# A two-network forward pass on one NeuronCore: side work of the delta-rule and sparse-attention branches moved by two to four places along the weight stream

## The chip, the core and the metric

The kernel runs on one core of one Trainium2 chip. The core has TensorE (PE, matrix products; its loading of weights is shown apart as PEld), VectorE (DVE), ScalarE (ACT), GpSimd (POOL) and SyncE (SP, which issues most transfers). The metric is the device time of one execution in microseconds; lower is better.

## The reference

Two networks run one after the other on the same 256 tokens of width 1024, each with two layers. The second one is the one that matters here. The core of its layer:

```python
h = rmsnorm(x, norm_mix[l])
(dq, dk, dv, dz, db, da, sq, sk, sv, iq, ik, iw, xq, gl) = jnp.split(h @ w_in[l], split_pts, axis=-1)
o_dn = deltanet_branch(dq, dk, dv, dz, db, da, conv_w[l], a_log[l], dt_bias[l], dn_norm[l])
o_sa = dsa_branch(sq, sk, sv, iq, ik, iw, positions)
o_xa = memory_branch(xq, rmsnorm(mem, norm_mem[l]), w_mem_kv[l])
gates = jax.nn.sigmoid(gl + b_gate[l])
merged = gates[:, :, 0] * (o_dn @ w_branch[l, 0]) + gates[:, :, 1] * (o_sa @ w_branch[l, 1]) + ...
x = x + merged @ w_out[l]
```

deltanet_branch: a causal convolution of width 4 and silu on q, k, v; per head (8 of them) and chunk of 64 tokens a unit lower triangular system is solved, and a state is carried from chunk to chunk; the output is normalised and multiplied by silu(z). dsa_branch: an index product relu(iq ik) weighted and summed over 8 index heads gives a score, the best 64 keys of each query are selected, and attention runs over these alone; q, k and iq carry a rotary embedding. memory_branch: plain attention over 256 memory rows. A gated feed-forward network follows. Everything is float32.

## The kernel before, in words

**The weight stream.** TensorE's main work is one long stream of matrix products with weights from device memory. A weight arrives in halves of 128x1024. Each is split in two: ScalarE writes the high part (w_hi, L339), GpSimd the remainder (w_lo, L348), and TensorE forms three products (x_hi w_hi, x_lo w_hi, x_hi w_lo; L147 to L149). A half is two parts of 12 matmuls of 256 columns (6 of 512 where the output is laid out by tokens, as in sv). Before w_hi of a half may be written, an earlier half's product must be done, since the buffers for halves are a ring.

**Units.** Halves are grouped into units, each with a target bank of PSUM and a follow-up on ScalarE or VectorE. In a layer of the second network, counted in halves from sm: sm 0-1; q0, q1, k0, k1, v0, v1, z0, z1 (2-17, first head half); q2 to z3 (18-33, second head half); sq 34-41; sk 42-49; iq 50-53; sv0 54-57; sv1 58-61; then gates and branch products by turns, gl00 62-63, wb00 64-65, gl01 66-67, wb01 68-69 and so on, and xq from 78. A part number is twice the half's.

**Side work.** All else on TensorE (the chunk solve, scan, index product, scores, transposes) is set between parts by hand. `main.pe(pe, n)` issues the stream up to part n; `main.act(...)` and `main.dve(...)` do the same for the follow-ups on their engines, so that the written order is the order in each engine's queue. An engine works through its queue in that order and waits on semaphores. For the delta rule `places` (L1541) makes a table of part numbers from a start and a list of gaps, one for each head half; the names are the steps: spread, spread_e, k0 ... g1 (preparation), lower (transposes of the start of the solve, two groups g of four head-chunks), y1, c1 ... y5, c5 (five levels of the solve, a product and a masked cross product each), solved, w0, o0 ... w3, o3 (scan of four chunks), tail0, tail1 (transposes of the result for two token tiles; its high and low part are o_dn_hi and o_dn_lo). For the sparse attention `self.at(half)` gives the places: index (L1804), scores (L1819), turn (L1831), weighted (L1841). On VectorE, index_sum (L2340) sums the eight index heads in eight operations into sc, index_mask (L2354) takes the best keys by repeated maximum and replacement; its dictionary says after which rounds the stream's follow-ups are issued and up to which half.

**Hooks.** The convolution of a q, k or v unit is two ScalarE operations and six of VectorE (L1384). The rotary embedding of sq, sk and iq is a small matmul two halves after the unit's end and three VectorE operations (L1575) three halves after it; iq1's stands at part 114. branch_unit adds gated products into acc on VectorE (L1489, "merged(k,n)"), which frees the bank of wb for the next one.

**Tables.** ScalarE needs a table load when it changes between function sets (Silu, Ln and Exp, and so on). `preload_act_table_set` puts one at a chosen place.

Of the kernel before, what the change touches and what calls it, by code (L numbers as in the profile page):

```python
# [1320 lines left out]
class Mixer2:  # L1321


    def __init__(self, net, l):
# [110 lines left out]
        for t in ("sq", "sk"):  # L1435
            for i in range(4):
                plain(f"{t}{i}", m[t][:, 2 * i:2 * i + 2, :], 5 - i % 2, rope=(j, "perm128", cs[:, 0, :], sn[:, 0, :]))
                j += 1
        for i in range(2):
            plain(f"iq{i}", m["iq"][:, 2 * i:2 * i + 2, :], 5 - i % 2, rope=(j, "perm64", cs[:, 1, :], sn[:, 1, :]))  # L1440
            j += 1
        for c in range(2):
            token_unit(f"sv{c}", m["sv"][:, :, c * HALF:(c + 1) * HALF], [4 + 2 * c, 5 + 2 * c], xs)
        u["sv1"].need = u["sv1"].need + [("rot_read", l, 9), ("rot_read", l, 10)]

# [82 lines left out]
        self.units = [u[n] for n in self.order]  # L1528
        self.steps = [self.places(0, 32), self.places(1, 76)]

# [10 lines left out]
    def places(self, hf, start):  # L1541

        gaps = ([("spread", 0), ("spread_e", 2 if hf == 0 else 1), ("k0", 2 if hf == 0 else 1), ("k1", 1), ("v0", 1), ("v1", 1), ("q0", 1), ("q1", 1), ("beta", 1),
                 ("g0", 1), ("g1", 1), ("lower0", 2), ("lower1", 1)] + [(f"{n}{lv}", 1) for lv in range(1, 6) for n in ("y", "c")]
                + [("solved", 1)] + [(f"{n}{c}", g) for c in range(NCH) for n, g in (("w", 2), ("o", 1))]
                + [("tail0", 4), ("tail1", 1)])
        at, out = start, {}
        for name, gap in gaps:
            at += gap
            out[name] = at  # L1550
        return out
# [35 lines left out]
    def pe(self, pe):  # L1587
# [28 lines left out]
        for hf in range(2):  # L1616
            self.prepare_pe(pe, hf)
            self.solve_pe(pe, hf)
            self.scan_pe(pe, hf, key_sum)
        self.index_pe(pe, 0, 60)  # L1620
        main.pe(pe, self.at(65))
        self.scores_pe(pe, 0)
        self.scores_pe(pe, 1)
        self.index_pe(pe, 1, 66)
        main.pe(pe, self.at(69))
        self.scores_pe(pe, 2)
        self.scores_pe(pe, 3)
        self.turn_pe(pe, 0)
        self.turn_pe(pe, 1)
        main.pe(pe, self.at(71))  # L1630
        self.weighted_pe(pe, 0)
        self.weighted_pe(pe, 1)
        main.pe(pe, self.at(78))
        self.turn_pe(pe, 2)
        main.pe(pe, self.at(79))
        self.turn_pe(pe, 3)
        main.pe(pe, self.at(80))
        self.weighted_pe(pe, 2)
        main.pe(pe, self.at(81))
        self.weighted_pe(pe, 3)  # L1640
        main.pe(pe, self.at(83))
        for g in (0, 1, 2):
# [80 lines left out]
    def solve_pe(self, pe, hf):  # L1723
        net, l, sig = self.net, self.l, self.net.sig
        K, main, m, bank = net.K, net.main, net.mem2, net.bank
        h = m["half"]
        yd, cp = bank[0:2], bank[2:4]
        for g in range(2):
            main.pe(pe, self.step_at(hf, f"lower{g}"))
            pe.wait_ge(*sig.at("begun", l, hf, g))  # L1730
            for n in range(4 * g, 4 * g + 4):
                mm = pe.transpose(yd[g][:, (n % 4) * P:(n % 4 + 1) * P], h["ti"][:, n, :], K("ident"))
            mm.then_inc(*sig.up("begun_turned", l, hf, g))
# [151 lines left out]
    def act(self, act):  # L1885
# [31 lines left out]
        for hf in range(2):  # L1917
            self.chain_act(act, hf, key_log)
        main.act(act, self.at(60))
        self.index_act(act, 0)  # L1920
        main.act(act, self.at(66))
        self.exponentials(act, 0)
        self.exponentials(act, 1)
        self.index_act(act, 1)
        main.act(act, self.at(69))
        self.turned_copy(act, 0)
        self.turned_copy(act, 1)
        main.act(act, self.at(71))
        self.weighted_high(act, 0)
        self.weighted_high(act, 1)  # L1930
        main.act(act, self.at(75))
        self.exponentials(act, 2)
        self.exponentials(act, 3)
        main.act(act, self.at(78))
        self.turned_copy(act, 2)
        main.act(act, self.at(79))
        self.turned_copy(act, 3)
        main.act(act, self.at(80))
        self.weighted_high(act, 2)
        act.preload_act_table_set("natural_log_exp_and_others")  # L1940
        for tt in range(TT):
# [28 lines left out]
    def chain_act(self, act, hf, key_log):  # L1970
# [4 lines left out]
        act.wait_ge(*sig.at("diffed", l, hf))  # L1975
        act.activation(h["e"][:, :, :], h["e"][:, :, :], ACT.Exp).then_inc(*sig.up("decay_made", l, hf))
        for g in range(2):
            main.act(act, self.step_at(hf, f"lower{g}"))
            act.wait_ge(*sig.at("begun_turned", l, hf, g))
            act.activation(h["t"][:, 4 * g:4 * g + 4, :], bank[g][:, :].rearrange("p (n i) -> p n i", n=4), ACT.Copy  # L1980
                           ).then_inc(*sig.up("t_begun", l, hf, g))
# [5 lines left out]
        for c in range(NCH):  # L1987
# [81 lines left out]
    def dve(self, dve):  # L2069
# [43 lines left out]
        for hf in range(2):  # L2113
            self.prepare_dve(dve, hf, unit_key)
            self.solve_dve(dve, hf)
            self.scan_dve(dve, hf, unit_key)
        main.dve(dve, self.at(60))
        self.index_sum(dve, 0)
        self.index_mask(dve, 0, {})
        main.dve(dve, self.at(65))  # L2120
        self.weigh(dve, 0)
        self.weigh(dve, 1)
        main.dve(dve, self.at(66))
        self.normalise(dve, 0)
        self.normalise(dve, 1)
        self.index_sum(dve, 1)
        self.index_mask(dve, 1, {1: 70})
        for g in (0, 1):
            self.weighted_low(dve, g)
        self.weigh(dve, 2)  # L2130
        main.dve(dve, self.at(74))
        self.weigh(dve, 3)
        self.normalise(dve, 2)
        self.normalise(dve, 3)
        dve.wait_ge(*sig.at("mem_loaded", l))
        bn, mv, ms = m["mem_bn"], m["mem_mv"], m["mem_ms"]
        for tt in range(TT):
            for half in range(2):
# [4 lines left out]
                                     ).then_inc(*sig.up("mem_var", l, tt))  # L2143
        main.dve(dve, self.at(80))
        self.weighted_low(dve, 2)
        for tt in range(TT):
            dve.wait_ge(*sig.at("mem_root", l, tt))
            dve.tensor_scalar(m["mem"][:, tt, :], m["mem"][:, tt, :], m["mem_rs"][:, tt:tt + 1], None, ALU.mult
                              ).then_inc(*sig.up("mem_normed", l, tt))
        main.dve(dve, self.at(81))  # L2150
        self.weighted_low(dve, 3)
        main.dve(dve, self.at(83))
        gain = prm(l, "norm_mem")
# [105 lines left out]
    def solve_dve(self, dve, hf):  # L2259
# [443 lines left out]
```

## Time and profile before

| | us |
|---|---|
| time, median of 3 runs | 2277.57 (2274.91 to 2277.58) |
| the profiled execution, its own time | 2277.58 |
| its span in the profile | 2275.8 |
| PE busy | 2163.2 (95%) |
| POOL busy | 1498.6 (66%) |
| ACT busy | 1073.0 (47%) |
| DVE busy | 955.9 (42%) |

The first network takes about 650 us. The attention part of the second network's first layer runs from 651 to 1075 us of the span, and the second layer's a little over 800 us later. Busy times are of the whole span. The granted clock is TensorE's share of full speed (2.4 GHz).

### The profile page before, as it was taken

The page shows a single profiled execution, that of the slowest core. Times are in us where ns is not written, and L with a number is a line of the kernel's source. Part 1 is how long each engine was busy: PE and PEld are TensorE (multiplying, and loading weights), DVE is VectorE, ACT ScalarE, POOL GpSimd, SP SyncE. Part 2 cuts the span into 40 slices and gives each one's busy share as a digit, 9 for nine tenths or more (in the row PEclk, how much of TensorE's full clock was granted, in tenths as well). Part 3 has the DMA queues.
Part 4 walks back from the last instruction along what each step waited for, and adds up shares of the span by engine and source line. Part 5 has one row for each costly group of instructions (what it writes and reads, how often), then busy time and mean ns, then how long its engine had stood idle before and what let it go on. Part 6 is the DMA issues. An engine that isn't in the chain of part 4 may idle for free.

```text
span 2275.8 us, 35984 instructions
## 1 busy us (share of the span) xinstructions
PE 2163.2 (95%) x15336; PEld 2001.3 (88%) x15336; DVE 955.9 (42%) x1484; ACT 1073.0 (47%) x1517; POOL 1498.6 (66%) x632
## 2 busy tenths in 40 slices
PE   8989989899969899999999899998999999999998
PEld 7789978799959888989999899898889899998998
DVE  4353256442375537477112211456374681123112
ACT  4555555555545352255444444473441454544444
POOL 6679877698846234356778688663243566786886
PEclk9999999999989999999999999999999999999999
DMA  8345544355524113134445455442131344454553
GB/s 338 132 146 204 185 139 161 117 180 187 184 84 147 60 71 106 64 128 167 151 164 185 148 185 185 156 145 90 56 112 56 130 148 149 157 182 150 184 185 133
DMA packets 47183, 333.05 MB, mean 146 GB/s; under 512 B 5168, under 2 KB 5552, under 8 KB 7856
## 3 DMA queue, kind: packets, MB, share of 16 engines
q1 hardware_dynamic: 47024, 330.76, 41.9%
q8 instruction: 121, 1.98, 0.4%
q14 instruction: 38, 0.31, 0.0%
HBM read 329.69 MB, written 1.05 MB: 145 GB/s over the span
## 4 chain that ended last, share of the span: by engine, by line
PE 62%; DVE 8%; issue 1%; ACT 1%; POOL 0%; DVEq 0%; ACTq 0%
PE bank L147 14%; PE bank L149 14%; PE bank L148 14%; PE y L147 2%; PE y L149 2%; PE y L148 2%; PE bank L1749 2%; PE bank L1748 1%; PE bank L1739 1%; DVE conv L1384 1%; PE bank L1672 1%; PE bank L1794 1%; PE bank L1791 1%; PE bank L1774 1%; DVE sq L1583 1%
## 5 line engine op out<-in xcount | busy, mean ns | idle before, releaser
L348 POOL TENSOR_TENSOR w_lo<-w_raw,w_hi 128x1024 fp32r<-128x1024 f32 x602 | 1463.0, 2437 | 759.7 <-ACT w_hi L339 759.6
L339 ACT ACTIVATE w_hi<-w_raw 128x1024 fp32r<-128x1024 f32 x602 | 635.7, 1059 | 1009.4 <-PE bank L149 838.9
L147 PE MATMUL bank<-x_hi,w_hi 128*128 128x256 f32 x2960 | 876.6, 296 | 21.6 <-POOL w_lo L348 17.1
L148 PE MATMUL bank<-x_lo,w_hi 128*128 128x256 f32 x2960 | 848.4, 287 | 0.0
L149 PE MATMUL bank<-x_hi,w_lo 128*128 128x256 f32 x2960 | 848.3, 287 | 0.0
L147 PEld LDWEIGHTS bank<-x_hi,w_hi 128*128 128x128 f32 x2960 | 579.1, 196 | 44.9 <-issue 24.4
L148 PEld LDWEIGHTS bank<-x_lo,w_hi 128*128 128x128 f32 x2960 | 579.0, 196 | 10.5 <-issue 8.6
L149 PEld LDWEIGHTS bank<-x_hi,w_lo 128*128 128x128 f32 x2960 | 578.4, 195 | 0.0
L876 DVE SCALAR_TENSOR_TENSOR conv<-bank,par_sb,conv 128x254 f32<-128x254 f32 (+1 forms) x176 | 76.8, 478 | 240.1 <-ACT conv L864 238.6
L1246 DVE TENSOR_TENSOR hid_lo<-hid,hid_hi 128x512 fp32r<-128x512 f32 x22 | 45.1, 2048 | 241.2 <-ACT hid_hi L1241 241.2
L147 PE MATMUL y<-w_hi,hid_hi 128*128 128x512 f32 x352 | 139.9, 397 | 3.3 <-DVE hid_lo L898 3.3
L149 PE MATMUL y<-w_hi,hid_lo 128*128 128x512 f32 x352 | 138.9, 395 | 0.0
L148 PE MATMUL y<-w_lo,hid_hi 128*128 128x512 f32 x352 | 138.9, 395 | 0.0
L1384 DVE SCALAR_TENSOR_TENSOR conv<-bank,par_sb,conv 128x255 f32<-128x255 f32 (+1 forms) x144 | 62.6, 477 | 63.8 <-ACT conv L1375 62.1
L147 PEld LDWEIGHTS y<-w_hi,hid_hi 128*128 128x128 f32 x352 | 66.3, 188 | 19.2 <-DVE hid_lo L898 5.4
L149 PEld LDWEIGHTS y<-w_hi,hid_lo 128*128 128x128 f32 x352 | 66.2, 188 | 15.7
L148 PEld LDWEIGHTS y<-w_lo,hid_hi 128*128 128x128 f32 x352 | 66.2, 188 | 13.8
L1491 DVE SCALAR_TENSOR_TENSOR gate<-gate,bank 128x512 f32<-128x512 f32 x16 | 11.0, 688 | 130.5 <-PE bank L149 130.5
L1749 PE MATMUL bank<-ti,es 128*128 128x128 f32 x320 | 61.0, 290 | 4.1 <-DVE es L2275 4.1
L1748 PE MATMUL bank<-es,ti 128*128 128x128 f32 x256 | 51.8, 286 | 7.0 <-DVE es L2275 7.0
L1749 PEld LDWEIGHTS bank<-ti,es 128*128 128x128 f32 x320 | 49.6, 205 | 4.5 <-DVE es L2275 4.5
L2347 DVE SCALAR_TENSOR_TENSOR sc<-index,tokq,sc 128x128 f32<-128x128 f32 (+1 forms) x28 | 52.6, 1878 | 1.0
(397 smaller groups left out, 3243.6 us busy)
## 6 DMA issues: line engine op xcount, KB each, us to landing
w_raw<-w SPq DMA_DIRECT2D x300, 1024.0 KB, 4.8
ln_rows<-ln_rows SPq DMA_DIRECT2D x4, 1024.0 KB, 7.2
mem_tok<-mem SPq DMA_DIRECT2D x2, 1024.0 KB, 4.9
const_sb<-const SPq DMA_DIRECT2D x1, 1536.0 KB, 9.3
par_sb<-par SPq DMA_DIRECT2D x2, 553.5 KB, 10.7
xn<-xT SPq DMA_DIRECT2D x1, 1024.0 KB, 4.9
w_raw<-w SPq DMA_DIRECT2D x2, 512.0 KB, 5.4
x_tok<-x SPq DMA_DIRECT2D x1, 1024.0 KB, 7.2
```

The lines of the kernel that those rows point to most:

```text
L147: pe.matmul(out, lhs[0], rhs[0], start=start, stop=False, skip_group_check=skip)
L148: pe.matmul(out, lhs[0], rhs[1], start=False, stop=False, skip_group_check=skip)
L149: return pe.matmul(out, lhs[1], rhs[0], start=False, stop=stop, skip_group_check=skip)
L339: act.activation(self.hi[:, h % HALVES, :], self.raw[:, n % RAWS, i * HW:(i + 1) * HW], ACT.Copy).then_inc(*sig.up("high", h))
L348: pool.tensor_tensor(self.lo[:, h % HALVES, :], self.raw[:, n % RAWS, i * HW:(i + 1) * HW], self.hi[:, h % HALVES, :].bitcast(F32), ALU.su ...
L876: ins = dve.scalar_tensor_tensor(cb[:, j, tap:T], view[:, j, 0:T - tap], taps[:, 2 - tap, c0 + j:c0 + j + 1], cb[:, j, tap:T], ALU.mult, A ...
L1246: dve.tensor_tensor(net.hs2[1][:, 2 * (i % 3):2 * (i % 3) + 2, :], m["hid"][:, i % 2, :, :], net.hs2[0][:, 2 * (i % 3):2 * (i % 3) + 2, :] ...
L1384: ins = dve.scalar_tensor_tensor(cb[:, j, tap:T], two(b)[:, j, 0:T - tap], taps[:, 3 - tap, c0 + j:c0 + j + 1], cb[:, j, tap:T], ALU.mult, ...
L1583: net.dve_chain.step(dve.tensor_tensor(raw, raw, cos.unsqueeze(1).to_broadcast([P, w, T]), ALU.mult))
L1748: pe.matmul(yd[g][:, c], h["ti"][:, n, :], h["y"][:, n, :], start=True, stop=True)
L1749: mm = pe.matmul(cp[g][:, c], h["y"][:, n, :], h["ti"][:, n, :], start=True, stop=True)
L2347: ins = dve.scalar_tensor_tensor(sc, m["r"][qt][:, (h % 2) * 4 + h // 2, :], m["tokq"][:, qt, 4, h:h + 1], mask if h == 0 else sc, ALU.mul ...
```

## The change

Places of the first head half start at part 30 and not 32, those of the second at 73 and not 76. The transposes of the solve, lower0 and lower1, become one place, lower, so that everything from y1 on is one part closer still. The banks of sq, sk and iq change from 5, 4 to 4, 5 by turns. sv1 no longer waits for the last two rotations to be read. Index product, scores, turn and weighted steps move to earlier halves. On ScalarE a call that issues the stream's follow-ups up to one part before tail0 is put ahead of the table preload of the tail. On VectorE index_mask(1) issues follow-ups at three rounds and not one, the call for half 66 before normalise(0) becomes 64, and that before weigh(3) moves behind normalise(2).

```diff
-                plain(f"{t}{i}", m[t][:, 2 * i:2 * i + 2, :], 5 - i % 2, rope=(j, "perm128", cs[:, 0, :], sn[:, 0, :]))
+                plain(f"{t}{i}", m[t][:, 2 * i:2 * i + 2, :], 4 + i % 2, rope=(j, "perm128", cs[:, 0, :], sn[:, 0, :]))
...
-        u["sv1"].need = u["sv1"].need + [("rot_read", l, 9), ("rot_read", l, 10)]
...
-        self.steps = [self.places(0, 32), self.places(1, 76)]
+        self.steps = [self.places(0, 30), self.places(1, 73)]
...
-                 ("g0", 1), ("g1", 1), ("lower0", 2), ("lower1", 1)] + [(f"{n}{lv}", 1) for lv in range(1, 6) for n in ("y", "c")]
+                 ("g0", 1), ("g1", 1), ("lower", 2)] + [(f"{n}{lv}", 1) for lv in range(1, 6) for n in ("y", "c")]
...
-        self.index_pe(pe, 0, 60)
-        main.pe(pe, self.at(65))
+        self.index_pe(pe, 0, 58)
+        main.pe(pe, self.at(63))
         self.scores_pe(pe, 0)
         self.scores_pe(pe, 1)
-        self.index_pe(pe, 1, 66)
-        main.pe(pe, self.at(69))
+        self.index_pe(pe, 1, 64)
+        main.pe(pe, self.at(67))
         self.scores_pe(pe, 2)
         self.scores_pe(pe, 3)
         self.turn_pe(pe, 0)
         self.turn_pe(pe, 1)
-        main.pe(pe, self.at(71))
+        main.pe(pe, self.at(69))
...
+        main.pe(pe, self.step_at(hf, "lower"))
         for g in range(2):
-            main.pe(pe, self.step_at(hf, f"lower{g}"))
...
+        main.act(act, self.step_at(hf, "tail0") - 1)
         act.preload_act_table_set("natural_log_exp_and_others")
...
-        main.dve(dve, self.at(66))
+        main.dve(dve, self.at(64))
         self.normalise(dve, 0)
         self.normalise(dve, 1)
         self.index_sum(dve, 1)
-        self.index_mask(dve, 1, {1: 70})
+        self.index_mask(dve, 1, {1: 66, 4: 69, 6: 70})
         for g in (0, 1):
             self.weighted_low(dve, g)
         self.weigh(dve, 2)
-        main.dve(dve, self.at(74))
         self.weigh(dve, 3)
         self.normalise(dve, 2)
+        main.dve(dve, self.at(75))
         self.normalise(dve, 3)
```

The later places (78 to 83 on three engines) move down by one half, the ScalarE and VectorE calls in step with TensorE's.

VectorE's queue in the first layer, from the maxima of weigh(1) to the first round of index_mask(1), before:

```order
L2379 TENSOR_SCALAR mx_190<-mx_190 128x4
L1489 SCALAR_TENSOR_TENSOR merged<-gate_171,bank 128x512
L2385 RECIPROCAL rc_192<-sum_191 128x4
L2386 TENSOR_TENSOR sm_0_158<-sm_0_158,rc_192 128x512
L2385 RECIPROCAL rc_192<-sum_191 128x4
L2386 TENSOR_TENSOR sm_1_159<-sm_1_159,rc_192 128x512
L2347 SCALAR_TENSOR_TENSOR sc<-index_154,tokq,const_sb 128x256
L2347 SCALAR_TENSOR_TENSOR sc<-index_154,tokq,sc 128x256 x7
L2362 MAX m_189<-sc 128x8
L2363 MATCH_REPLACE wk<-m_189,sc 128x256
L1489 SCALAR_TENSOR_TENSOR merged<-gate_171,bank 128x512
```

The first merged is merged(0,0), the second merged(0,1). The same stretch of VectorE's queue after the change:

```order
L2379 TENSOR_SCALAR mx_190<-mx_190 128x4
L2385 RECIPROCAL rc_192<-sum_191 128x4
L2386 TENSOR_TENSOR sm_0_158<-sm_0_158,rc_192 128x512
L2385 RECIPROCAL rc_192<-sum_191 128x4
L2386 TENSOR_TENSOR sm_1_159<-sm_1_159,rc_192 128x512
L2347 SCALAR_TENSOR_TENSOR sc<-index_154,tokq,const_sb 128x256
L2347 SCALAR_TENSOR_TENSOR sc<-index_154,tokq,sc 128x256 x7
L2362 MAX m_189<-sc 128x8
L2363 MATCH_REPLACE wk<-m_189,sc 128x256
L1488 SCALAR_TENSOR_TENSOR merged<-gate_171,bank 128x512
```

merged(0,0) has moved behind the sum and the first round; merged(0,1) comes three rounds later.

VectorE's queue at the end of the second head half, a piece of the difference (the rope of iq1 against the tail and the first index sum):

```order
 L2326 TENSOR_TENSOR mt<-vb,o_ms 128x512 x2
-L1582 TENSOR_TENSOR rope_148<-bank,tables 128x512
-L1583 TENSOR_TENSOR iq<-iq,tables 128x512
-L1585 TENSOR_TENSOR iq<-iq,rope_148 128x512
+L1581 TENSOR_TENSOR rope_148<-bank,tables 128x512
+L1582 TENSOR_TENSOR iq<-iq,tables 128x512
+L1584 TENSOR_TENSOR iq<-iq,rope_148 128x512
 L2332 SCALAR_TENSOR_TENSOR o_turned<-bank,par_sb,z_set_112 128x512 x2
 L2338 TENSOR_TENSOR o_dn_lo<-o_turned,o_dn_hi 128x4x128 x2
+L1581 TENSOR_TENSOR rope_148<-bank,tables 128x512
+L1582 TENSOR_TENSOR iq<-iq,tables 128x512
+L1584 TENSOR_TENSOR iq<-iq,rope_148 128x512
```

Ahead of the tail stood the rope of iq1 and stands now that of iq0; iq1's is the last of the piece, behind o_dn_lo.

ScalarE's queue at the end of the first head half, from the last copy of the scan on, after the change:

```order
L1994 ACTIVATE vb<-bank 64x512
L1998 ACTIVATE mt<-vb 128x512
L339 ACTIVATE w_hi<-w_raw 128x1024
L1399 ACT_TABLE_LOAD
L1399 ACTIVATE z_set_112<-bank 128x512
L339 ACTIVATE w_hi<-w_raw 128x1024
L2001 ACT_TABLE_LOAD
L2005 ACTIVATE o_ms<-o_ms,const_sb 128x4
L2008 ACTIVATE o_ms<-o_ms 128x4
```

And before:

```order
L1995 ACTIVATE vb<-bank 64x512
L1999 ACTIVATE mt<-vb 128x512
L2001 ACT_TABLE_LOAD
L2005 ACTIVATE o_ms<-o_ms,const_sb 128x4
L2008 ACTIVATE o_ms<-o_ms 128x4
```

The Silu of z3 (z_set_112), its table load and two w_hi stand between the scan and the tail's table load now; before, the same Silu was issued ahead of the last vb copy.

## Rows read from the trace of the kernel before

**Rows 1.** The page, part 1: busy us, share of span, instructions.

```profile
PE 2163.2 (95%) x15336; PEld 2001.3 (88%) x15336; DVE 955.9 (42%) x1484; ACT 1073.0 (47%) x1517; POOL 1498.6 (66%) x632
```

**Rows 2.** Waits of PE, 651 to 1075: us in total, times, longest.

```profile
PE bank L1732 <- DVE ti L2256: 5.3, 2, 3.1
...
PE bank L1748 <- DVE es L2275: 3.5, 2, 2.0
PE bank L147 <- DVE merged L1489: 2.6, 2, 1.4
PE bank L1749 <- DVE es L2275: 2.0, 1, 2.0
PE bank L1785 <- DVE v_new L2304: 1.7, 1, 1.7
```

**Rows 3.** Stretches: length, busy us (instructions) by engine, PEclk, DMA share, GB/s.

```profile
703.00:857.00 154.00, 143.59 (x1051) 134.84 (x1050) 75.64 (x134) 72.65 (x100) 58.34 (x25) 0.92 0.24 81
857.00:990.00 133.00, 130.78 (x956) 116.62 (x954) 81.78 (x117) 38.97 (x52) 50.99 (x22) 1.00 0.26 90
1080.00:1105.00 25.00, 25.00 (x212) 25.00 (x212) 0.00 (x1) 11.45 (x14) 20.69 (x9) 1.00 0.49 169
1512.00:1666.00 154.00, 143.66 (x1059) 134.44 (x1058) 75.85 (x135) 73.35 (x100) 59.73 (x25) 0.93 0.25 85
```

**Rows 4.** Timeline of ACT: start, us, instructions, [idle before, releaser].

```profile
707.26 0.67 ACT L1891 ACTIVATE keys<-bank,const_sb 128x512 f32<-128x512 f32 x1
...
840.15 1.06 ACT L339 ACTIVATE w_hi<-w_raw 128x1024 fp32r<-128x1024 f32 x1 [1.09 <-PE bank L149]
...
842.52 0.60 ACT L1399 ACTIVATE z_set<-bank 128x512 f32<-128x512 f32 x1
...
848.33 1.28 ACT L2001 ACT_TABLE_LOAD   x1
```

**Rows 5.** Timeline of PE, side work of the first layer.

```profile
708.83 0.91 PE L1672 MATMUL bank<-rowq,const_sb 8*128 8x256 f32 x3
...
854.68 0.60 PE L1801 MATMUL bank<-const_sb,mt 128*128 128x128 f32 x4
...
984.39 0.60 PE L1801 MATMUL bank<-const_sb,mt 128*128 128x128 f32 x4
...
989.03 1.16 PE L1815 MATMUL bank<-ik,iq 64*128 64x128 f32 x16
...
1019.87 3.70 PE L1827 MATMUL index<-sk,sq 128*128 128x256 f32 x16
...
1024.20 0.36 PE L147 MATMUL bank<-o_dn_hi,w_hi 128*128 128x256 f32 x1
```

**Rows 6.** Timeline of DVE, first layer.

```profile
741.81 2.69 DVE L1384 SCALAR_TENSOR_TENSOR conv<-bank,par_sb,conv 128x255 f32<-128x255 f32 x6 [1.11 <-ACT conv L1375]
...
745.85 2.71 DVE L2256 TENSOR_TENSOR ti<-const_sb,ti 128x512 f32<-128x512 f32 x1
...
850.20 1.29 DVE L2326 TENSOR_TENSOR mt<-vb,o_ms 128x512 f32<-128x512 f32 x2 [1.16 <-ACT o_ms L2008]
...
855.99 1.76 DVE L2338 TENSOR_TENSOR o_dn_lo<-o_turned,o_dn_hi 128x512 fp32r<-128x512 f32 x2
...
980.72 0.69 DVE L1582 TENSOR_TENSOR rope<-bank,tables 128x512 f32<-128x512 f32 x1
...
984.20 2.77 DVE L1585 TENSOR_TENSOR iq<-iq,rope 128x512 f32<-128x512 f32 x1
...
1019.83 0.49 DVE L2347 SCALAR_TENSOR_TENSOR sc<-index,tokq,const_sb 128x256 f32<-128x256 f32 x1 [0.91 <-ACT index L2022]
...
1020.35 13.90 DVE L2347 SCALAR_TENSOR_TENSOR sc<-index,tokq,sc 128x256 f32<-128x256 f32 x7
...
1035.27 0.69 DVE L1489 SCALAR_TENSOR_TENSOR merged<-gate,bank 128x512 f32<-128x512 f32 x1
```

**Rows 7.** Timeline of POOL beside the second index sum.

```profile
1020.82 7.42 POOL L348 TENSOR_TENSOR w_lo<-w_raw,w_hi 128x1024 fp32r<-128x1024 f32 x3 [8.07 <-ACT w_hi L339]
```

More of the change, by code:

```diff
@@ L1436, in __init__ @@
             for i in range(4):
-                plain(f"{t}{i}", m[t][:, 2 * i:2 * i + 2, :], 5 - i % 2, rope=(j, "perm128", cs[:, 0, :], sn[:, 0, :]))
+                plain(f"{t}{i}", m[t][:, 2 * i:2 * i + 2, :], 4 + i % 2, rope=(j, "perm128", cs[:, 0, :], sn[:, 0, :]))
                 j += 1
         for i in range(2):
-            plain(f"iq{i}", m["iq"][:, 2 * i:2 * i + 2, :], 5 - i % 2, rope=(j, "perm64", cs[:, 1, :], sn[:, 1, :]))
+            plain(f"iq{i}", m["iq"][:, 2 * i:2 * i + 2, :], 4 + i % 2, rope=(j, "perm64", cs[:, 1, :], sn[:, 1, :]))
             j += 1
@@ L1629, in pe @@
         self.turn_pe(pe, 1)
-        main.pe(pe, self.at(71))
+        main.pe(pe, self.at(69))
         self.weighted_pe(pe, 0)
         self.weighted_pe(pe, 1)
+        main.pe(pe, self.at(77))
+        self.turn_pe(pe, 2)
         main.pe(pe, self.at(78))
-        self.turn_pe(pe, 2)
+        self.turn_pe(pe, 3)
         main.pe(pe, self.at(79))
-        self.turn_pe(pe, 3)
+        self.weighted_pe(pe, 2)
         main.pe(pe, self.at(80))
-        self.weighted_pe(pe, 2)
-        main.pe(pe, self.at(81))
         self.weighted_pe(pe, 3)
-        main.pe(pe, self.at(83))
+        main.pe(pe, self.at(82))
         for g in (0, 1, 2):
@@ L1918, in act @@
             self.chain_act(act, hf, key_log)
-        main.act(act, self.at(60))
+        main.act(act, self.at(58))
         self.index_act(act, 0)
-        main.act(act, self.at(66))
+        main.act(act, self.at(64))
         self.exponentials(act, 0)
@@ L1924, in act @@
         self.index_act(act, 1)
-        main.act(act, self.at(69))
+        main.act(act, self.at(67))
         self.turned_copy(act, 0)
         self.turned_copy(act, 1)
-        main.act(act, self.at(71))
+        main.act(act, self.at(69))
         self.weighted_high(act, 0)
@@ L1933, in act @@
         self.exponentials(act, 3)
+        main.act(act, self.at(77))
+        self.turned_copy(act, 2)
         main.act(act, self.at(78))
-        self.turned_copy(act, 2)
+        self.turned_copy(act, 3)
         main.act(act, self.at(79))
-        self.turned_copy(act, 3)
-        main.act(act, self.at(80))
         self.weighted_high(act, 2)
@@ L1947, in act @@
                            ).then_inc(*sig.up("mem_root", l, tt))
-        main.act(act, self.at(81))
+        main.act(act, self.at(80))
         self.weighted_high(act, 3)
-        main.act(act, self.at(83))
+        main.act(act, self.at(82))
         gain = net.prm2(l, "norm_mem")
@@ L1976, in chain_act @@
         act.activation(h["e"][:, :, :], h["e"][:, :, :], ACT.Exp).then_inc(*sig.up("decay_made", l, hf))
+        main.act(act, self.step_at(hf, "lower"))
         for g in range(2):
-            main.act(act, self.step_at(hf, f"lower{g}"))
             act.wait_ge(*sig.at("begun_turned", l, hf, g))
@@ L2116, in dve @@
             self.scan_dve(dve, hf, unit_key)
-        main.dve(dve, self.at(60))
+        main.dve(dve, self.at(58))
         self.index_sum(dve, 0)
         self.index_mask(dve, 0, {})
-        main.dve(dve, self.at(65))
+        main.dve(dve, self.at(63))
         self.weigh(dve, 0)
         self.weigh(dve, 1)
-        main.dve(dve, self.at(66))
+        main.dve(dve, self.at(64))
         self.normalise(dve, 0)
@@ L2143, in dve @@
                                      ).then_inc(*sig.up("mem_var", l, tt))
-        main.dve(dve, self.at(80))
+        main.dve(dve, self.at(79))
         self.weighted_low(dve, 2)
@@ L2149, in dve @@
                               ).then_inc(*sig.up("mem_normed", l, tt))
-        main.dve(dve, self.at(81))
+        main.dve(dve, self.at(80))
         self.weighted_low(dve, 3)
-        main.dve(dve, self.at(83))
+        main.dve(dve, self.at(82))
         gain = prm(l, "norm_mem")
@@ L2267, in four @@
             return bank[b][:, :].rearrange("p (n i) -> p n i", n=4)
-        main.dve(dve, self.step_at(hf, "lower1"))
+        main.dve(dve, self.step_at(hf, "lower"))
         for lv in range(1, 6):
```

## The prediction

> **What bounds the kernel now.** I read the page's first part first: TensorE is busy for 2163.2 of the 2275.8 us span [rows 1]. No other engine comes near that, so the time can only change through what TensorE waits for and through its clock. The second view is TensorE's waits in the attention part of the second network's first layer, 651 to 1075 us, the only code that the diff touches. The relevant waits there are short and few [rows 2]: 5.3 us before the transposes of the solve (L1732), 3.5 and 2.0 us before its products (L1748, L1749), 1.7 us in the scan (L1785) and 2.6 us for merged; together 15.1 us. The third view is the table of stretches [rows 3]. From 703 to 857 us (first head half, solve and scan) the granted clock is 0.92, from 857 to 990 us it is 1.00, with only 2.2 us of waits (5.3 less 3.1, [rows 2]). The second layer's first stretch has 0.93 and the same busy time, so I work one layer out and double it. In a stretch without side work 212 matmuls take 25.00 us [rows 3], 0.118 us each, so a part of 12 matmuls takes 1.42 us. This is the unit in which every place of the change converts to time.
>
> The change issues the same matmuls. It moves side work against the weight stream, by 2 to 4 parts, so each step costs or gives what the chains on ScalarE and VectorE then leave TensorE waiting for. All waits below are per layer.
>
> **The first head half, places two or three parts earlier.**
> - Spread, now at part 30. It needs the second logarithm of the keys, which ends at 707.26 + 0.67 = 707.93 [rows 4]. TensorE starts the spread at 708.83 today [rows 5]; two parts earlier is 708.83 - 2.84 = 706.0. A wait of 2.0 us that isn't there now.
> - The transposes ("lower", both groups at one place) and y1. Today the second group waits 3.1 us [rows 2]: a convolution hook of 2.69 us (741.81) stands ahead of it on VectorE, so that its last operation, L2256, runs from 745.85 for 2.71 us, to 748.56 [rows 6]. In the new order the hook falls behind the group. What ends last then is the copy of t on ScalarE for y1, and a table load of 1.28 us [rows 4] no longer falls before it. I take 1.7 us in place of 3.1.
> - The levels c2 and c4. The convolution hook (2.69 us [rows 6]) falls in two of the five levels, and VectorE's masked product is behind it. Three such waits cost 1.5, 2.0 and 2.0 today. I count two at the mean of these less the part that lies ahead of the hook, 1.45 each: 2.9 in place of 5.5.
> - The scan. w and o are closer to z2 and the key logarithms; o0 0.5 and o1 1.85 in place of 1.7.
> - sq0. Its bank was 5 and becomes 4, which z3 has just filled. ScalarE first does w_hi (from 840.15), then a table load and the Silu, which ends at 842.52 + 0.60 = 843.12 [rows 4]. TensorE has nothing to do in that time but sq0: 843.12 - 840.15 plus a signal, 3.1 us, new.
> - tail0, now at part 71. The new call ahead of the preload puts z3's Silu and one more w_hi ahead of the table load, and that w_hi waits for the product that ends at part 70. From there: w_hi 1.06, load 1.28 and the two small operations that follow it (848.33 to 850.20 [rows 4, 6]), the first half of VectorE's 1.29 us, and 0.3 for signals: 3.9 us. TensorE gets there after one part with a little side work, 1.5 us. New wait 2.4 us.
>
> **The second head half.**
> - Its transposes: one rope step fewer stands ahead on VectorE. 0.7 in place of 2.2.
> - tail0 at 112: the same ScalarE chain of 3.9 us, but two parts (2.84 us) of cover: 1.1, new.
> - index0 at part 116. The index product needs the rope of iq1, whose hook stays at part 114. Today it is ahead of the tail on VectorE (980.72 on [rows 6]) and index0 waits for nothing. With the tail at 112 and 113 VectorE takes the tail first. From tail1's transposes (854.68 [rows 5]) to the end of the second o_dn_lo (855.99 + 1.76 [rows 6]) are 3.1 us; then the rope, which took 984.20 + 2.77 - 980.72 = 6.2 us here and would take 2.1 as three operations of 0.69 us. TensorE goes from tail1 (984.39) to index0 (989.03) in 4.6 us [rows 5]. So 3.1 + 6.2 - 4.6 = 4.7 at most and 0.6 at least. I take 4.2, since the rows at that very place are the slow ones.
> - wb01, now the largest term. It overwrites the bank from which merged(0,0) reads. Today that addition stands ahead of the second index sum, after the change behind it. From index0 to the start of that sum 1019.83 - 989.03 = 30.8 us pass [rows 5, 6]. That stretch is a chain on VectorE and ScalarE (top-k, weights, exponentials), so it keeps its length when both move; less the addition that leaves it, 30.1. From the start of the sum to the end of the addition that follows its first maximum is 1035.27 + 0.69 - 1019.83 = 16.1 us: merged(0,0) is done 46.2 us after index0. TensorE's way from index0 (part 116) to part 136 is 20 parts. Today's 18 parts to 138 took 1019.87 - 989.03 = 30.84 [rows 5]; two more are 2.84, and the scores and transposes that now come at 134 are 1024.20 - 1019.87 = 4.3: 38.0. That leaves 8.2 us. VectorE's sums are slow, 13.90 / 7 = 1.99 us each against 0.49 for the first, while GpSimd makes w_lo beside them [rows 6, 7]. While TensorE stands still GpSimd soon runs out of work, and the last sums should be fast. I take 6.5; ends 4.0 and 8.2. The two waits for merged that are there today (2.6) go.
>
> What lies later (memory attention, turn and weighted steps 2 and 3, moved by one half) showed no wait and has many parts of cover; I cost it at nothing. If that is wrong it is one more wait like the others, 1 to 2 us.
>
> VectorE and GpSimd both show it: 0.49 us against 1.99 for the same operation [rows 6]. The Trainium skill, "SBUF — State Buffer", section "Who interferes with whom", says that a VectorE operation with two SBUF inputs and a GpSimd one that reads SBUF take turns on one port pair for a whole instruction each. The trace agrees; by that rule the last sums run free once GpSimd has stopped, which speaks for 6.5 and against 8.2.
>
> **The sum.** After: 2.0 + 1.7 + 2.9 + 2.35 + 3.1 + 2.4 + 0.7 + 1.1 + 4.2 + 6.5 = 26.95 us per layer. Before: 15.1. The difference is 11.8, for two layers 23.7 us.
>
> The clock comes on top. In the stretch of clock 0.92, 8% of 154 us is 12.3 us lost beside 154 - 143.59 = 10.4 us of waits [rows 3], so about 1.2 us of clock per us of waiting. The new waits of that stretch are 14.4, 4.0 more: 4.7 us. In the second half the clock stays at 1.00 with 4.8 us of waits spread over 200 us; 12.5 us of waits could cost nothing or 1.2 per us of the added 7.7 (9 us). I take 2. So 6.7 us per layer, 13.4 for both. 23.7 + 13.4 = 37 us.
>
> The profiled execution took 2277.58 us, 1.8 more than its span, and is within 0.01 us of the median, so nothing is to be converted: 2277.6 + 37 = 2315 us.
>
> **The rivals.**
> 1. The same signs, but VectorE catches up. With ropes at 0.69 us each the index wait is 0.6, wb01's 4.0, the second half's transposes wait nothing, and the clock in the second half stays at 1.00: 19.6 - 15.1 = 4.5, plus 2 of clock, times two: 13 us, 2291. For it: whenever TensorE stops, GpSimd stops. Against: the stop begins only after the slow operations.
> 2. The clock falls in the second half too, as it did in the first. Then 11.8 + 4.7 + 9 = 25.5 per layer, 2329. For it: 12.5 us of waits, more than the first stretch has today. Against: they are two separate holes, not many.
> 3. Faster. One mechanism: VectorE's eight index sums run beside an idle GpSimd. At 0.49 us they take 3.9 instead of 14.4 us, so merged(0,0) is ready before TensorE arrives; with the rope equally fast both terms of the second half go. 26.95 - 10.7 is 16.2, and if sq0's and tail0's waits, three parts apart, share one delay, 13.8: 1.3 less than today, with the clock's share 2.9 per layer, 2272. It decides at sums of 0.8 us each (14.4 less the 8.2 of the wait, over eight, leaves 0.8). Against: GpSimd's 7.42 us block of three w_lo lies beside the sums [rows 7].
> 4. No change: the gains in solve and scan balance a smaller loss.
> 5. Table loads cost more than their rows. From the end of w_hi at 841.21 to the start of the Silu at 842.52 are 1.31 us, a load of 1.28 and next to nothing behind it [rows 4], and I used that. The Trainium skill, "ScalarE: Activation LUTs", section "What ACT_TABLE_LOAD costs", gives a drain of about 1.4 us on top. By that, as an estimate, sq0 and both tails would wait 1.4 us longer each, 4.1 per layer, 8 in all: 2323. The sum doesn't use it.
>
> **How the numbers follow.** Forecast (2300 to 2322) 0.42; rival 1 (2283 to 2300) 0.23; rival 2 (2322 to 2345) 0.23; rival 3 0.04; rival 4 0.04; rival 5 0.04. A change of under 0.2%, 4.5 us, can't be told from none. So faster 0.04, same 0.04, slower 0.92. The range 2293 to 2340 takes in the bounds of wb01 and of the index wait and leaves out the ends of rivals 1 and 2.
>
> **What the profile after would show.** A wait of 5 to 8 us of TensorE for merged at about part 136 in each layer, one of some 4 us for the rope before L1815, 3 us for z_set before the first matmul of sq, 2 us before the spread (keys, ScalarE), and 2.4 us before the tail (L1800, VectorE's mt). The three waits before L1747/L1748 shrink to two. The clock from 703 us on stays near 0.9 or falls a little. I'd be wrong if merged(0,0) is not waited for, or if the index sums after the change take under 8 us: then rival 3 or 1 holds. I'd be wrong on the clock if 857 to 990 falls below 0.98.

## The result, and the profile after

The changed kernel takes 2318.73 us (median of 4 runs, 2318.51 to 2325.93) against 2277.57 before. The ratio is 1.0182, with a 95% interval of 1.0169 to 1.0196: slower by 41 us. The profiled execution has a span of 2315.0 us, 39.2 more than before.

The first part of the page of the changed kernel, which answers to [rows 1]:

```profile
PE 2173.9 (94%) x15336; PEld 2008.9 (87%) x15336; DVE 945.6 (41%) x1484; ACT 1076.2 (46%) x1519; POOL 1499.2 (65%) x632
```

TensorE is busy for 10.7 us more with the same 15336 matmuls, so 10.7 of the 39.2 us are slower matmuls and the other 28.5 are waiting. The waits of TensorE from 651 to 1095 us, the same code as in [rows 2] (us in total, times, longest):

```profile
PE bank L1731 <- DVE ti L2256: 6.2, 3, 3.4
PE bank L1814 <- DVE iq L1584: 5.3, 1, 5.3
PE bank L147 <- DVE merged L1488: 4.8, 2, 2.5
...
PE bank L1800 <- DVE mt L2326: 4.1, 2, 2.7
PE bank L147 <- ACT z_set L1399: 3.1, 1, 3.1
PE bank L1784 <- DVE v_new L2304: 2.2, 2, 1.9
PE bank L1671 <- ACT keys L1890: 2.0, 1, 2.0
PE bank L1738 <- DVE e L2284: 1.7, 2, 0.8
```

These are 29.4 us in the first layer, where [rows 2] had 15.1: 14.3 more. (The row left out at the dots is a wait of 4.8 us for w_lo that both kernels have.) In the second layer the list is the same within 0.1 us. Twice 14.3 is 28.6, all the waiting that was added. The two kinds of wait of the levels (es, 5.5 us in [rows 2]) have shrunk to the last row, 1.7 us; that is the change's only gain.

The single waits on TensorE's timeline (the number in brackets is the idle time before the row, with its releaser):

```profile
707.24 0.56 PE L1671 MATMUL bank<-rowq,const_sb 8*128 8x256 f32 x1 [1.96 <-ACT keys L1890]
...
748.32 0.59 PE L1731 MATMUL bank<-const_sb,ti 128*128 128x128 f32 x2 [3.43 <-DVE ti L2256]
...
845.27 0.58 PE L147 MATMUL bank<-x_hi,w_hi 128*128 128x256 f32 x1 [3.12 <-ACT z_set L1399]
...
999.87 0.59 PE L1814 MATMUL bank<-ik,iq 64*128 64x128 f32 x2 [5.32 <-DVE iq L1584]
...
1042.04 0.58 PE L147 MATMUL bank<-o_dn_hi,w_hi 128*128 128x256 f32 x1 [2.35 <-DVE merged L1488]
...
1070.95 0.39 PE L147 MATMUL bank<-o_dn_hi,w_hi 128*128 128x256 f32 x1 [2.47 <-DVE merged L1488]
```

VectorE's timeline at the places that the readings below rest on, the first transposes, the first index sum (1003.50) and the second (from 1030.02):

```profile
741.40 2.78 DVE L2256 TENSOR_TENSOR ti<-const_sb,ti 128x512 f32<-128x512 f32 x1
...
745.54 2.72 DVE L2256 TENSOR_TENSOR ti<-const_sb,ti 128x512 f32<-128x512 f32 x1
...
1003.50 2.68 DVE L2347 SCALAR_TENSOR_TENSOR sc<-index,tokq,sc 128x128 f32<-128x128 f32 x7
...
1018.14 0.69 DVE L2375 TENSOR_TENSOR sm<-bank,mask 128x512 f32<-128x512 f32 x1 [5.32 <-PE bank L1826]
...
1030.02 0.48 DVE L2347 SCALAR_TENSOR_TENSOR sc<-index,tokq,const_sb 128x256 f32<-128x256 f32 x1 [0.91 <-ACT index L2022]
...
1030.54 9.74 DVE L2347 SCALAR_TENSOR_TENSOR sc<-index,tokq,sc 128x256 f32<-128x256 f32 x7
...
1041.30 0.69 DVE L1488 SCALAR_TENSOR_TENSOR merged<-gate,bank 128x512 f32<-128x512 f32 x1
```

The seven operations of the first index sum take 2.68 us here. In the kernel before they took 12.81:

```profile
992.57 12.81 DVE L2347 SCALAR_TENSOR_TENSOR sc<-index,tokq,sc 128x128 f32<-128x128 f32 x7
```

In the changed kernel GpSimd had stood idle for 8.07 us, up to 1007.33, so these seven ran alone; before, it was busy beside them. The second row below is ScalarE's, from the time of the scores:

```profile
1007.33 2.41 POOL L348 TENSOR_TENSOR w_lo<-w_raw,w_hi 128x1024 fp32r<-128x1024 f32 x1 [8.07 <-ACT w_hi L339]
...
1021.89 1.06 ACT L339 ACTIVATE w_hi<-w_raw 128x1024 fp32r<-128x1024 f32 x1 [3.60 <-PE bank L149]
```

Stretches of the changed kernel, with the granted clock as the third number from the end:

```profile
837.00:842.00 5.00, 5.00 (x41) 4.47 (x39) 1.44 (x3) 3.00 (x5) 1.61 (x1) 1.00 0.00 0
845.30:852.30 7.00, 6.99 (x36) 6.78 (x36) 0.00 (x0) 1.42 (x2) 0.73 (x2) 0.60 0.43 150
1001.90:1008.00 6.10, 6.10 (x24) 4.95 (x23) 4.43 (x16) 2.15 (x3) 0.67 (x1) 0.79 0.24 99
703.00:862.00 159.00, 143.34 (x1017) 132.39 (x1015) 81.03 (x135) 72.00 (x98) 54.98 (x23) 0.90 0.22 73
862.00:990.00 128.00, 124.30 (x925) 112.85 (x925) 72.06 (x108) 34.78 (x45) 49.32 (x21) 0.99 0.24 83
990.00:1042.00 52.00, 44.36 (x287) 39.60 (x284) 35.94 (x66) 25.60 (x45) 27.98 (x12) 0.93 0.40 137
```

Just before sq0 the clock is 1.00. In the 7 us behind the 3.12 us wait it is 0.60, and 36 matmuls take 7.0 us, where 36 at the 0.122 us each of the stretch just before take 4.4. Behind the 5.32 us wait of index0 it is 0.79 for 6 us. Half of full speed is the lower level, 1.2 GHz. So a wait of 3 to 5 us is followed by some microseconds in which part of the matmuls run at half speed. In the second half (990 to 1042) the mean is 0.93, where [rows 3] had 1.00 up to 990 and before's clock stayed at 1.00 after it.

### The profile page after: what moved, and what is told of

It is laid out like the page before. It is cut to its first block, busy times and chain, and to the rows that moved or that the text cites. A ratio compares the mean times of both kernels' runs of the same rounds, so it can differ in the third digit from the quotient of the medians.

```text
span 2315.0 us, 35984 instructions
## 1 busy us (share of the span) xinstructions
PE 2173.9 (94%) x15336; PEld 2008.9 (87%) x15336; DVE 945.6 (41%) x1484; ACT 1076.2 (46%) x1519; POOL 1499.2 (65%) x632
## 4 chain that ended last, share of the span: by engine, by line
PE 60%; DVE 8%; ACT 3%; issue 2%; POOL 0%; DVEq 0%; ACTq 0%
PE bank L147 14%; PE bank L149 13%; PE bank L148 13%; PE y L147 2%; PE y L149 2%; PE y L148 2%; PE bank L1738 2%; PE bank L1748 1%; DVE conv L1384 1%; PE bank L1747 1%; PE bank L1671 1%; DVE sc L2347 1%; PE bank L1790 1%; PE bank L1793 1%; PE bank L1566 1%
## 5 line engine op out<-in xcount | busy, mean ns | idle before, releaser
L147 PE MATMUL bank<-x_hi,w_hi 128*128 128x256 f32 x2960 | 878.7, 297 | 27.8 <-POOL w_lo L348 17.1
L147 PE MATMUL bank<-w_hi,x_hi 128*128 128x512 f32 x128 | 53.4, 417 | 0.0
L148 PE MATMUL bank<-w_lo,x_hi 128*128 128x512 f32 x128 | 50.9, 398 | 0.0
L149 PE MATMUL bank<-w_hi,x_lo 128*128 128x512 f32 x128 | 50.7, 396 | 0.0
```

The costliest lines, as they stand in the source:

```text
L147: pe.matmul(out, lhs[0], rhs[0], start=start, stop=False, skip_group_check=skip)
L148: pe.matmul(out, lhs[0], rhs[1], start=False, stop=False, skip_group_check=skip)
L149: return pe.matmul(out, lhs[1], rhs[0], start=False, stop=stop, skip_group_check=skip)
```

## The experiments

All times are medians. The kernel before ran beside each of them on the same chip (2277.6 to 2278.0 us), and the intervals are of the ratio to it. "U" below is the changed kernel.

### One edit of the change undone

**The banks (u_bank).** sq, sk and iq use banks 5, 4 by turns as before.

```diff
-plain(f"{t}{i}", ..., 4 + i % 2, rope=...)
+plain(f"{t}{i}", ..., 5 - i % 2, rope=...)
```

> The changed kernel with sq, sk and iq in banks 5, 4 by turns as before; all else changed. Theory: the 3.12 us wait for z_set before sq0 in each layer, and the slow clock behind it (36 matmuls in 7.02 us, 2.5 us more than at 0.126 each), vanish, and tail0's wait of 2.65 us stays: 5.6 per layer, 11 us less than the changed kernel, about 2308. Rival: ScalarE's chain, not the bank, is the limit, and the delay only moves to tail0, whose wait grows to over 5 us: 2316 or more.

Measured 2307.99 us, ratio 1.0133 (1.0119 to 1.0147), 10.7 less than U. The wait for z_set is gone, and tail0 waits as long as before, 2.7 us:

```profile
851.21 0.66 PE L1800 MATMUL bank<-const_sb,mt 128*128 128x128 f32 x4 [2.74 <-DVE mt L2326]
```

The theory holds to within 0.3 us. A bank costs what its last reader is behind, and here also 5.4 - 3.1 = 2.3 us of slow matmuls per layer.

**iq1's rope ahead of the second tail (u_rope).**

```diff
-        self.u[name].hooks = {("pe", 2): pe, ("dve", 3): dve}
+        self.u[name].hooks = {("pe", 2): pe, ("dve", 2 if name == "iq1" else 3): dve}
```

> The changed kernel with iq1's rope on VectorE one hook earlier (at part 112, ahead of the second tail's o_turned). Theory: index0's wait falls from 5.3 to between 0 and 2.5 us and the slow stretch behind it (72 matmuls in 15.1 us, 6 us more than at 0.126 each) goes; merged(0,0) takes back 0 to 2.6 us per layer: 17 to 22 us less than the changed kernel, about 2299. Rival: the clock behind the wait was slow for another reason and only the wait goes, 5 per layer: 2308.

Measured 2323.7 us, ratio 1.0207 (1.0193 to 1.0221): 5 us slower than U by the medians, though the two intervals touch, and in any case not faster. Both theories fall. The waits of the first layer:

```profile
PE bank L147 <- DVE merged L1488: 9.1, 2, 6.7
...
PE index L1826 <- ACT index L2022: 1.8, 1, 1.8
...
PE bank L1814 <- DVE o_turned L2332: 0.2, 1, 0.2
```

index0 waits 0.2 us in place of 5.3, but merged 9.1 in place of 4.8, and 1.8 more come at the scores. VectorE's rows at the first and the second sum:

```profile
1000.84 12.81 DVE L2347 SCALAR_TENSOR_TENSOR sc<-index,tokq,sc 128x128 f32<-128x128 f32 x7
...
1026.65 0.48 DVE L2347 SCALAR_TENSOR_TENSOR sc<-index,tokq,const_sb 128x256 f32<-128x256 f32 x1 [0.91 <-ACT index L2022]
...
1027.17 11.85 DVE L2347 SCALAR_TENSOR_TENSOR sc<-index,tokq,sc 128x256 f32<-128x256 f32 x7
...
1040.05 0.69 DVE L1488 SCALAR_TENSOR_TENSOR merged<-gate,bank 128x512 f32<-128x512 f32 x1
```

index0 starts at 994.34 here, so merged(0,0) ends 1040.05 + 0.69 - 994.34 = 46.4 us later; in U the same chain took 1041.30 + 0.69 - 999.87 = 42.1 us. So index0 comes 5.5 us earlier, and merged(0,0) only 1.3 us. The trace shows where the rest went: without the wait of index0 GpSimd doesn't stop, and the first index sum takes 12.81 us again and not 2.68. Whoever lets TensorE arrive earlier at the head of this chain makes it wait longer at its end.

**merged(0,0) ahead of the second sum (u_wb).**

```diff
-        main.dve(dve, self.at(64))
+        main.dve(dve, self.at(66))
         self.normalise(dve, 0)
```

> The changed kernel with merged(0,0) ahead of the second index sum on VectorE, as before. Theory: the first wait for merged (2.35 us) and about 1.4 us of slow clock behind it go in each layer, the second (2.47) stays: 7 us less than the changed kernel, about 2312. Rival: VectorE now holds up its queue for the product of half 65, the sum begins later and the wait moves to the scores or to the next merged: no change, 2318.

Measured 2318.09 us, ratio 1.0178 (1.0164 to 1.0191): no change, as the rival said, but not for its reason. The first of the two waits for merged is gone (2.5 us in all and not 4.8), although VectorE now waits 7.35 us for the product:

```profile
1030.72 0.69 DVE L1488 SCALAR_TENSOR_TENSOR merged<-gate,bank 128x512 f32<-128x512 f32 x1 [7.35 <-PE bank L149]
```

From index0 to the memory scores TensorE needs 128.5 us in both layers (1129.4 - 1000.9 in the first) where U needs 132.5 (1132.4 - 999.9), so the edit brings 4.0 us per layer where it acts. It is given back elsewhere: the traced execution is 2.1 us longer than U's, so some 10 us come back, and 7 of them in one stretch. In the second layer, scan and preparation of the second half, first with the edit, then U:

```profile
1630.00:1689.00 59.00, 50.97 (x331) 44.66 (x330) 21.98 (x39) 35.08 (x48) 20.29 (x9) 0.88 0.20 72
1689.00:1725.00 36.00, 36.00 (x224) 31.86 (x223) 27.59 (x37) 8.76 (x10) 14.08 (x7) 0.86 0.25 89
```

```profile
1633.00:1689.00 56.00, 47.95 (x331) 41.59 (x330) 21.16 (x39) 34.31 (x47) 19.04 (x9) 0.94 0.22 76
1689.00:1721.00 32.00, 32.00 (x230) 28.61 (x229) 28.46 (x37) 9.64 (x12) 16.14 (x7) 1.00 0.29 100
```

The same stretch of work with the same idle time of TensorE (59 - 50.97 and 56 - 47.95, 8.0 us each) runs at a clock of 0.88 and 0.86 where U has 0.94 and 1.00, and takes 7 us more. Nothing was changed in that stretch, and U's own first layer, with the same code, has 0.86 over its like (800 to 860). Why the clock differs isn't settled.

**Both edits on VectorE (u_rope_wb).**

> The changed kernel with both edits on VectorE: iq1's rope ahead of the second tail, and merged(0,0) ahead of the second index sum. Theory: the wait of index0 and that of wb01 are two ends of one chain from the tail to merged(0,0), so one edit alone moves the wait and only both shorten it: index0 as with the rope edit alone (0.2), no wait for merged(0,0) (6.65 with the rope edit alone), 8 to 9 us less per layer than the changed kernel, about 2301. Rival: the chain's end only moves on to the scores or to merged(0,1) and the time stays over 2312.

Measured 2307.04 us, ratio 1.0128 (1.0112 to 1.0145): 11.7 less than U, where the two alone gave -0.6 and +5.0. The theory of one chain holds: each end alone brings nothing, both together 11.7. Its size was given too large (2301), since waits remain at the scores and at the later merged:

```profile
PE bank L147 <- DVE merged L1488: 3.1, 2, 2.8
...
PE index L1826 <- ACT index L2022: 1.8, 1, 1.8
```

**And the banks (u_three).**

> As the one before, with the banks 5, 4 of sq, sk and iq as well. Theory: the bank's share is independent of the chain in the second half, so another 10.7 us go as with the bank edit alone: about 2291; what is left over the kernel before are the waits before the spread, the transposes and the tails. Rival: the tail's wait takes the bank's back once the rest is short, 2300.

2295.86 us, ratio 1.0081 (1.0068 to 1.0094): 11.2 less again. The bank's share is independent of the chain, 10.7 alone and 11.2 here.

**And without the new call ahead of the tail's table preload (u_tail).**

```diff
-        main.act(act, self.step_at(hf, "tail0") - 1)
         act.preload_act_table_set("natural_log_exp_and_others")
```

> The changed kernel with the two edits on VectorE and the banks as before, and now also without the new call on ScalarE ahead of the tail's table preload. Theory: the waits for mt before both tails (4.2 us per layer) and the slow matmuls behind them (0.9 us) go, 10 us less than with the call, about 2286. Rival: w_hi of two halves stands behind the scan's copies on ScalarE then, and TensorE waits for w_lo instead: 2293 or more.

2288.09 us, ratio 1.0046 (1.0034 to 1.0059): 7.8 less, nearly the 10 that were expected; the waits for mt are gone, and index0 waits 0.6 in place of 0.2 us.

**And the first half at 32 again (u_tail_32).**

```diff
-        self.steps = [self.places(0, 30), self.places(1, 73)]
+        self.steps = [self.places(0, 32), self.places(1, 73)]
```

> As u_tail, with the first head half starting at 32 again (so that y stands at odd places still, since lower is one place). Theory: the wait of the spread (2.0 us) and 1.6 us of slow clock behind it go per layer, the levels stay at 1.7: 7 us less than u_tail, about 2279. Rival: the transposes' wait (6.2 with the second half's 2.2) grows with it, no gain.

2278.14 us, ratio 1.0004 (0.9995 to 1.0013): 10 less, the kernel before again within its spread. Its waits sum to 14.9 us in the first layer against 15.1. The levels' gain of 3.8 us is still there, and 1.7 in the scan; they are eaten by 1.8 us at the scores, 0.6 at index0, 2.0 before the last products of the solve and 1.2 before a transpose of the preparation. The second group of transposes waits 4.5 us, where with the same start and two places it waited 3.1 [rows 2]: 1.4 more, the one part that the single place `lower` takes away.

### One thing done to the kernel before

**The first half at 31, or at 33 (b_31, b_33).**

```diff
-        self.steps = [self.places(0, 32), self.places(1, 76)]
+        self.steps = [self.places(0, 31), self.places(1, 76)]
```

> The kernel before with the first head half starting at part 31, nothing else. Theory: the place of the levels against the convolution hooks decides their waits; odd places of y give 1.7 us in all in place of 5.5, the transposes wait about 2 in place of 3.1, the spread 0.5 (new): 4.4 us per layer and some clock, 9 to 16 us less than before, about 2266. Rival: the levels' waits in the changed kernel shrank because both groups of transposes are issued together; then only the transposes gain, 2277.

> The kernel before with the first head half one part later (33), nothing else. Theory: what start 31 gained (20.6 us) came from odd places of y, so that the convolution hook at even parts falls between other steps, and 33 has the same: waits for es and e together about 1.7 per layer in place of 5.5, 2258 to 2266. Rival: earlier is what helped (the transposes waited less too); then 33 is no better than before, 2275 to 2290.

31: 2257.44 us, ratio 0.9911 (0.9898 to 0.9925). 33: 2258.34 us, ratio 0.9916 (0.9903 to 0.9930). Both are 20 us faster, so it isn't the direction of the shift but odd against even: y1 stands at 48 before, at 47 and 49 here, and at 45 in U; the hooks stand at 44, 48, 52 and so on. No other even place was tried. VectorE's timeline of the kernel before at the first level, where the hook stands ahead of es, for which TensorE waits next:

```profile
753.61 2.69 DVE L1384 SCALAR_TENSOR_TENSOR conv<-bank,par_sb,conv 128x255 f32<-128x255 f32 x6 [5.05 <-ACT conv L1375]
...
756.21 1.28 DVE L2275 TENSOR_TENSOR es<-bank,const_sb 128x512 f32<-128x512 f32 x2
```

And with start 31, where it stands ahead of ti and e of the same level, which are wanted only after the cross products:

```profile
753.39 2.68 DVE L1384 SCALAR_TENSOR_TENSOR conv<-bank,par_sb,conv 128x255 f32<-128x255 f32 x6 [2.62 <-ACT conv L1375]
...
756.59 0.68 DVE L2284 TENSOR_TENSOR e<-e,bank 128x512 f32<-128x512 f32 x1
```

The waits with start 31, first layer:

```profile
PE bank L1732 <- DVE ti L2256: 3.3, 2, 2.2
PE bank L147 <- DVE merged L1489: 2.5, 2, 1.4
PE bank L1756 <- DVE ti L2282: 2.0, 1, 2.0
PE bank L1739 <- DVE e L2284: 1.7, 2, 0.8
```

And with start 33:

```profile
PE bank L1739 <- DVE e L2284: 1.7, 2, 0.8
```

es is gone from both; e costs 1.7 us. With 33 the first hook stands ahead of es too, but TensorE comes for es one part later and finds it done. The waits sum to 10.0 us with 31 (with 0.5 for the spread) against 15.1, so about 5 of the 10 us per layer are waits. The rest is the clock, 0.97 over the first half, where [rows 3] have 0.92 and U 0.90:

```profile
703.00:862.00 159.00, 153.58 (x1151) 142.23 (x1151) 89.06 (x155) 79.40 (x106) 67.49 (x28) 0.97 0.26 92
```

u_tail_32 has y1 at 47 like this kernel and the same waits in the levels, and is 20.7 us slower. So what it still has of the change costs as much as the phase of the hooks brings: its waits are 4.9 us per layer more (14.9 against 10.0), at the scores (1.8), the transposes (1.2) and the preparation (1.2) above all.

**With start 31: merged(0,2) ahead of weigh(2) (b_31_m74), then the second half at 75 (best_75), then merged(0,1) ahead of the first round of maxima (best_75_m70):**

```diff
+        main.dve(dve, self.at(74))
         self.weigh(dve, 2)
-        main.dve(dve, self.at(74))
...
-        self.steps = [self.places(0, 31), self.places(1, 76)]
+        self.steps = [self.places(0, 31), self.places(1, 75)]
...
-        self.index_mask(dve, 1, {1: 70})
+        main.dve(dve, self.at(70))
+        self.index_mask(dve, 1, {})
```

> The kernel before with start 31 and merged(0,2) issued on VectorE ahead of weigh(2) in place of behind it. Theory: the wait of 1.41 us for it goes in each layer, 3 us less than start 31 alone, about 2254.5. Rival: weigh(2) is late by it and the turn step waits instead: 2257.

> The kernel before with starts 31 and 75 and merged(0,2) ahead of weigh(2). Theory: one part earlier in the second half takes the rope from ahead of the second group of transposes on VectorE, so its wait of 2.2 us goes and 0 to 1 is left; nothing else is late: 3 to 4 us less than with 76, about 2252. Rival: the tail or the index product takes the wait back: 2256 or more.

> As best_75, with merged(0,1) straight behind the second index sum, ahead of the first round of maxima. Theory: its wait of 1.0 us shrinks to about 0.1, 2 us less than best_75, about 2250. Rival: VectorE waits there for the product of half 69 and the top-k is late: 2252 or more.

2256.01 (ratio 0.9903, 0.9885 to 0.9921), 2252.32 (0.9891, 0.9878 to 0.9905) and 2252.67 us (0.9893, 0.9880 to 0.9907). The first gains 1.4 us, within its spread; the second took the 2.2 us wait out as expected (its 3.7 us over the first are within that one's spread, the 5.1 us over start 31 alone are not); the third changes nothing, since the gate on ScalarE and the later scores are then waited for. The second is the best version, 25.6 us below the kernel before. Its longest waits in the first layer:

```profile
PE bank L1756 <- DVE ti L2282: 2.0, 1, 2.0
PE bank L1739 <- DVE e L2284: 1.7, 2, 0.8
PE bank L1732 <- DVE ti L2256: 1.1, 1, 1.1
PE bank L147 <- DVE merged L1489: 1.0, 1, 1.0
```

## Why the prediction was right

The forecast was 2315 us, 37 more than before; it was 2318.7, 41 more. The sign holds, and so does the kind of cause: TensorE waits at the places that were named, and the clock adds to it. That the size came so close is in part luck. The sum's two parts were 23.7 us of waits (measured 28.6) and 13.4 us of clock (measured 10.7), and within the waits the largest term was too large by 4.2 us per layer while others were too small by 8.0 together. By its own steps, us per layer:

| step | forecast | measured |
|---|---|---|
| spread | 2.0 | 1.96 |
| transposes and y1, first half | 1.7 | 4.0 (0.55 + 3.43) |
| levels | 2.9 | 1.7 |
| scan | 2.35 | 2.2 |
| sq0 | 3.1 | 3.12 |
| tail0, first half | 2.4 | 2.65 |
| transposes, second half | 0.7 | 2.2 |
| tail0, second half | 1.1 | 1.5 |
| index0 | 4.2 | 5.3 |
| merged(0,0) | 6.5 | 2.35 |
| a later merged | 0 | 2.47 |
| sum | 26.95 | 29.4 |

- Spread, sq0 and both tails: right as worked out from rows. u_tail_32, u_bank and u_tail show them one by one. No table load cost more than its 1.28 us: the sq0 wait of 3.12 leaves no room for the 1.4 us more that the Trainium skill, "ScalarE: Activation LUTs", section "What ACT_TABLE_LOAD costs", gives for a drain. Rival 5 falls.
- The transposes failed in size and direction: 1.7 in place of 3.1 was forecast, and it grew to 4.0. I held that the hook's leaving frees the second group. The hook did leave, but with both groups at one place the part of 1.4 us between them went too (u_tail_32 shows that part by itself), and VectorE's last operation was slow for each group, 2.78 and 2.72 us (741.40 and 745.54 above), where before it was slow for the second alone ([rows 6]; the first took 0.69 us). In the second half no rope stands between the groups any more, as forecast, and the wait stayed at 2.2. u_tail_32, with the same places there, has no such wait in its first layer and 2.2 in its second; what decides it is open.
- The levels gained more than I forecast, and I named the hook but not the rule: behind the product of y it costs 1.5 to 2.0 us, ahead of ti and e 0.84.
- index0, 5.3 us, lies above the 4.7 that I gave as the most: the rope of iq0 stood ahead of the tail's operations on VectorE, so that the last o_dn_lo came 4.0 us after tail1's transposes and not 3.1.
- merged(0,0), the largest term, 2.35 us in place of 6.5 and below my lower end of 4.0; the wait of 5 to 8 us that I named as the sign isn't there. It and index0 were each worked out as if the other weren't there. I took it that the stretch from index0 to the second sum keeps its length. It seems to: 30.1 us forecast, 1030.02 - 999.87 = 30.15 measured. But that is luck, for it is made of other parts. The wait of index0 stopped GpSimd, and the first index sum took 2.68 us and not 12.81. TensorE ran at a clock of 0.87 behind the wait and reached the scores 17.1 us after index0 (15.0 in u_rope, at 1.00), so VectorE, ready early, waited 5.32 us for them (1018.14), 2.1 of these by the clock. ScalarE then began the exponentials at 1024.99 only, behind a w_hi (1021.89), a table load and the gate. The second sum took 9.74 us and not 13.90 [rows 6], and TensorE reached wb01 39.8 us after index0 and not 38.0. So the wait was 42.1 - 39.8 = 2.3.
- In u_rope, without the first wait, the second is 6.65 us, near the 6.5 forecast, again by parts that offset each other: 32.3 us to the sum (30.1 forecast), 14.1 from there (16.1) and 39.8 of TensorE's way (38.0, and 1.8 at the scores).
- A later merged, 2.47 us: I let both waits of [rows 2] go. The follow-up for half 74 stands behind normalise(2) now, which I had put down to nothing.
- The clock: I took 4.7 us per layer in the first half and 2 in the second. It was 5.4 in all. The first half fell from 0.92 to 0.90 (703 to 862), and the second did not stay at 1.00. Rival 2's sign was right there, not its size.

Rival 1 (VectorE catches up whenever GpSimd stops) is half true: both sums were shorter, the first by 10 us. Its own sum was also wrong: with its three terms it is 26.95 - 3.6 - 2.5 - 0.7 = 20.15 and not 19.6, so 2292 us. Rival 3 is excluded by the time: it wanted both waits of the second half at nothing, and only the two edits together come near. But the fast sums that it rested on were there, in the first sum.

## What to carry to other kernels

Count waits on one chain of engines once: here moving the head of the chain moved the wait to its end, and undoing one of the two edits alone showed nothing or worse. A wait of TensorE here also stopped GpSimd, and so made VectorE's sum faster; a forecast that adds waits one by one misses that. A match of two totals shows little until their parts match. A periodic follow-up (here every fourth part on VectorE) has a good and a bad phase against a periodic side chain; one place of shift, either way, brought 20 us, more than any other single edit tried. Before a bank changes hands, ask what its last reader's engine does ahead of the read.

## What the runs showed of the hardware

The clock makes waits dearer than they are. A wait of 3.12 us from full clock was followed by 7 us at a mean of 0.60, 2.6 us lost; a wait of 5.32 us by 6 us at 0.79. For the same stretch with the same waits it can come out differently, 0.86 against 1.00 over 32 to 36 us in two kernels that don't differ there. This swing of 7 us is as large as some of the edits tested, and covered most of a local gain of 4.0 us per layer.

Seven operations of the index sum on VectorE (128x128) took 12.81 us beside a busy GpSimd and 2.68 us while it stood idle.
